# Whole-number comparison, one masking step and one sum in the top-16 selection of a hybrid encoder step

## The reference, cut to what matters

```python
v1, i1 = lax.top_k(s1, PEER_TOPK)
v2, i2 = lax.top_k(s2, PEER_TOPK)
cand_s = (v1[..., :, None] + v2[..., None, :]).reshape(T, PEER_HEADS, PEER_TOPK * PEER_TOPK)
cand_i = (i1[..., :, None] * N_KEYS + i2[..., None, :]).reshape(T, PEER_HEADS, PEER_TOPK * PEER_TOPK)
top_s, sel = lax.top_k(cand_s, PEER_TOPK)
e_idx = jnp.take_along_axis(cand_i, sel, axis=-1)
gate = jax.nn.softmax(top_s, axis=-1)
u = exp_u[e_idx]
act = jax.nn.gelu(jnp.einsum('thkd,td->thk', u, h).astype(jnp.float32), approximate=False)
return jnp.einsum('thk,thkd->td', (gate * act).astype(h.dtype), exp_v[e_idx])
```

## Time and profile before

| | us |
|---|---|
| median of 3 runs | 1144.43 |
| lowest and highest | 1144.29, 1145.9 |
| the profiled execution, time | 1144.88 |
| its span | 1143.1 |

### The profile page before, as it was taken

One profiled execution on the slowest core, in us unless ns is written; L12 is line 12 of the kernel. 1 busy time (PEld: TensorE's weight loads), 2 busy tenths in 40 slices (PEclk: granted clock), 3 DMA queues, 4 the chain that ended last, 5 costly groups with the idle time before them and its releaser, 6 DMA issues.

```text
span 1143.1 us, 12068 instructions
## 1 busy us (share of the span) xinstructions
PE 856.5 (75%) x3879; PEld 396.3 (35%) x3884; DVE 784.8 (69%) x2005; ACT 454.8 (40%) x1423; POOL 536.3 (47%) x437
## 2 busy tenths in 40 slices
PE   8999988997896858685686777587666756655555
PEld 6748743443232424241243442143223222211111
DVE  2325877876677888796666786757877777667554
ACT  2121454333444334552564663343343333333334
POOL 0002445553555554553553553556564654455442
PEclk9999999999999888897889898889898788887879
DMA  9902999999999999999999999999999999999996
GB/s 375 411 2 70 421 425 425 427 424 430 425 427 425 426 428 426 361 430 422 425 427 425 425 427 427 425 426 427 426 427 426 427 427 428 427 425 427 427 428 269
DMA packets 66791, 456.60 MB, mean 399 GB/s; under 512 B 8227, under 2 KB 10019, under 8 KB 15526
## 3 DMA queue, kind: packets, MB, share of 16 engines
q0 software_dynamic: 55888, 402.68, 83.8%
q1 hardware_dynamic: 10694, 52.87, 11.4%
q10 hardware_dynamic: 144, 0.26, 0.1%
HBM read 451.49 MB, written 3.24 MB: 398 GB/s over the span
## 4 chain that ended last, share of the span: by engine, by line
DMA 48%; PE 26%; DVE 11%; POOL 7%; ACT 4%; issue 3%; SPq 0%; POOLq 0%; DVEq 0%
DMA rows<-in_uv,ids 37%; PE ps L598 25%; DMA wt<-in_uv,ids 8%; DVE rows L2043 6%; POOL rows L537 4%; POOL work L520 2%; DMA wt<-in_uv,last_ids 1%; DMA rows<-in_w_qi 1%; ACT work L1249 1%; ACT wt L1249 1%; DMA wt<-in_w_q 1%; ACT wgt L1249 1%; DVE wt L2043 1%; PE ps L601 1%; ACT zact L1249 1%
## 5 line engine op out<-in xcount | busy, mean ns | idle before, releaser
L537 POOL DMA_INDIRECT rows<-in_uv,ids x352 | 400.3, 1137 | 444.9 <-PE ps L598 360.7
L598 PE MATMUL ps<-rows,work 128*64 128x512 f32 x1416 | 409.4, 707 | 245.2 <-ACT work L1249 239.7
L2043 DVE CUSTOM_DVE_ANT_0 rows<-rows,wt 128x1024 f32<-128x1024 f32 x226 | 276.9, 1225 | 160.9 <-DMA rows<-in_uv,ids 155.7
L1249 ACT ACTIVATE zact<-zdot 128x1 f32<-128x1 f32 x354 | 71.6, 202 | 488.2 <-DVE zdot L2043 480.5
L598 PEld LDWEIGHTS ps<-rows,work 128*64 128x64 f32 x1416 | 96.2, 151 | 479.3 <-ACT work L1249 327.3
L598 PE MATMUL ps<-wt 128*128 128x128 f32 (+6 forms) x719 | 195.9, 476 | 30.4 <-ACT wt L1249 28.1
L2043 DVE CUSTOM_DVE_ANT_0 rows<-rows,masks 128x1024 f32<-128x1024 f32 x128 | 156.3, 1224 | 67.3 <-DMA rows<-in_uv,ids 64.5
L598 PEld LDWEIGHTS ps<-wt 128*128 128x128 f32 (+2 forms) x724 | 97.8, 185 | 106.6 <-issue 58.8
L1249 ACT ACTIVATE work<-pair,wgt 128x64 f32<-128x64 f32 x354 | 123.4, 349 | 11.5
L1249 ACT ACTIVATE wgt<-zact,gates 128x1 f32<-128x1 f32 x354 | 104.5, 295 | 11.6
L598 PEld LDWEIGHTS ps<-work,wt 128*128 128x128 f32 (+1 forms) x664 | 84.2, 202 | 48.6 <-issue 48.2
(11 more groups left out here) (178 smaller groups left out, 722.9 us busy)
## 6 DMA issues: line engine op xcount, KB each, us to landing
wt<-in_w_q SPq DMA_DIRECT2D x7, 2048.0 KB, 15.9
rows<-in_uv,ids POOLq DMA_INDIRECT x352
rows<-in_w_out SPq DMA_DIRECT2D x2, 2048.0 KB, 32.5
wt<-in_w_out SPq DMA_DIRECT2D x2, 2048.0 KB, 12.0
wt<-in_ckv SPq DMA_DIRECT2D x16, 256.0 KB
x<-in_x SPq DMA_DIRECT2D x5, 512.0 KB, 8.9
rows<-in_w_qi SPq DMA_DIRECT2D x1, 2048.0 KB, 13.3
wt<-in_w_qa SPq DMA_DIRECT2D x1, 2048.0 KB, 12.5
```

The costliest lines, as they stand in the source:

```text
L537: pool.indirect_dma_start(row[s], None, a["uv"], bass.IndirectOffsetOnAxis(ap=ids[:, own(n // KP).start + n % KP:own(n // KP).start + n % ...
L598: return nc.tensor.matmul(out, lhsT, rhs, start=start, stop=stop)
L1249: return nc.scalar.activation(*args, **kw)
L2043: V.tensor_tensor_reduce(row[s][:, 0:D], row[s][:, 0:D], h2r[t][:, n % 2, :], 1.0, 0.0, ALU.mult, ALU.add, zdots[s]).then_inc(dotted, 1)
```

## The change

- `topi` stays whole numbers: the cast to `topf` is gone. Its first half is shifted left by 7 (times 128) in place, by an instruction that is put behind the first maximum of the sums, with one wait for both.
- The shift, the mask and the cast of `besti` become one masking instruction, `besti` against the constants 240 and 15 (`nibble`, set at the start). The comparison is with 0, 16, .. 240 for the first half and 0..15 for the second (`iota`, now 2 x 16 and in another place).
- The one-hot table is multiplied by `topi` and summed over both halves and the last axis at once, straight into `flat`.
- Unit 0 posts `chosen` when its ids are there and again when its gates are; PE spreads them in two batches (`spread_first`), DVE posts `picked` after the ids and again after the gates, and POOL's first gather waits for the ids alone. All later counts of `chosen`, `spread_ps` and `picked` go up by one.
- `post` is `across` without the wait. It is used for `smax`, `pscaled` and the ids of units 1 to 23.

```diff
-        iota = sb("iota", [P, KP])
-        topf = at(work, 4000, 32).rearrange("p (e k) -> p e k", e=2)
+        nibble = at(work, 4000, 2).bitcast(U32)
-        rankf = at(work, 4096, 32).rearrange("p (e k) -> p e k", e=2)
-        half_id = at(work, 3840, 32).rearrange("p (e k) -> p e k", e=2)
+        iota = at(work, 4096, 32).rearrange("p (e k) -> p e k", e=2)
...
                 if n % KP == 0:
-                    pool.wait_ge(picked, n // KP + 1)
+                    pool.wait_ge(picked, n // KP + 2 if n else 1)
...
+            def spread_first():
+                pe.wait_ge(q_sb, 1)
+                for k in range(2):
+                    pe.wait_ge(chosen, k + 1)
+                    for j in range(2):
+                        for q in range(2):
+                            last = mm(spread_psum(k)[64 * q:64 * q + 64, j * KP + k * 8:j * KP + k * 8 + 8], ident[:, 64 * j:64 * j + 64],
+                                      flat[0].rearrange("p e (c q) -> p e q c", q=2)[:, k, q, :])
+                    last.then_inc(spread_ps, 1)
...
             sums_1(1)
-            spread_out(0)
+            spread_first()
             sums_1(2)
...
+            def post(ins, s):
+                key = s.name
+                count[key] = count.get(key, 0) + 1
+                ins.then_inc(s, 1)
+                yield
...
             def top16_pairs(u):
-                then(V.tensor_copy(topf, topi))
                 c4 = cand.rearrange("p (i j) -> p i j", i=KP)
...
-                then(V.max(out=best[:, 0:8], in_=cand))
+                V.max(out=best[:, 0:8], in_=cand).then_inc(chain, 1)
+                V.tensor_scalar(topi[:, 0, :], topi[:, 0, :], 7, None, ALU.logical_shift_left).then_inc(chain, 1)
+                count[chain.name] += 2
+                dve.wait_ge(chain, count[chain.name])
...
             def top16_ids(u):
-                V.tensor_scalar(rank[:, 0, :], besti, 4, None, ALU.logical_shift_right)
-                then(V.tensor_scalar(rank[:, 1, :], besti, 15, None, ALU.bitwise_and))
-                yield from across(V.tensor_copy(rankf, rank))
-                yield from across(V.tensor_tensor(hot, rankf.rearrange("p e (k a) -> p e k a", a=1).broadcast_to([P, 2, KP, KP]),
-                                                  iota[:].rearrange("p (e a r) -> p e a r", e=1, a=1).broadcast_to([P, 2, KP, KP]),
+                yield from across(V.tensor_tensor(rank, besti.rearrange("p (e k) -> p e k", e=1).broadcast_to([P, 2, KP]),
+                                                  nibble.rearrange("p (e k) -> p e k", k=1).broadcast_to([P, 2, KP]), ALU.bitwise_and))
+                yield from across(V.tensor_tensor(hot, rank.rearrange("p e (k a) -> p e k a", a=1).broadcast_to([P, 2, KP, KP]),
+                                                  iota.rearrange("p e (a r) -> p e a r", a=1).broadcast_to([P, 2, KP, KP]),
                                                   ALU.is_equal))
-                yield from across(V.tensor_tensor(hot, hot, topf.rearrange("p e (a r) -> p e a r", a=1).broadcast_to([P, 2, KP, KP]),
+                yield from across(V.tensor_tensor(hot, hot, topi.rearrange("p e (a r) -> p e a r", a=1).broadcast_to([P, 2, KP, KP]),
                                                   ALU.mult))
-                yield from across(V.tensor_reduce(half_id, hot, AX.X, ALU.add))
-                V.scalar_tensor_tensor(flat[u % 2][:, 0, :], half_id[:, 0, :], float(NK), half_id[:, 1, :], ALU.mult, ALU.add).then_inc(chain, 1)
-                count[chain.name] += 1
+                ids_of = V.tensor_reduce(flat[u % 2][:, 0, :], hot.rearrange("p e k r -> p k e r"), AX.XY, ALU.add)
+                if u == 0:
+                    ids_of.then_inc(chosen, 1)
+                else:
+                    yield from post(ids_of, chain)
...
             def spread_take(u):
-                dve.wait_ge(spread_ps, u + 1)
+                dve.wait_ge(spread_ps, u + 2 if u else 1)
                 src = spread_psum(u).rearrange("p (j e c) -> p e c j", j=2, e=2)
-                V.tensor_copy(ids[:, own(u)].rearrange("p (c j) -> p c j", j=2), src[:, 0, :, :])
-                if u >= 1:
-                    dve.wait_ge(picked, u)
+                ins = V.tensor_copy(ids[:, own(u)].rearrange("p (c j) -> p c j", j=2), src[:, 0, :, :])
+                if u == 0:
+                    ins.then_inc(picked, 1)
+                    dve.wait_ge(spread_ps, 2)
+                    src = spread_psum(1).rearrange("p (j e c) -> p e c j", j=2, e=2)
+                dve.wait_ge(picked, u + 1)
                 V.tensor_copy(gates[:, own(u)].rearrange("p (c j) -> p c j", j=2), src[:, 1, :, :]).then_inc(picked, 1)
...
             then(V.memset(ident_bf[:], 0.0), blank)
+            for i, bits in enumerate((240, 15)):
+                ins = V.memset(nibble[:, i:i + 1], bits)
+            then(ins)
```

## The result

The changed kernel took **1158.06 us** (1157.85 to 1158.81), the kernel before 1144.98 in the same comparison. The ratio is 1.0115, with a 95% interval of 1.0097 to 1.0132. The forecast was 1143.6 with a range to 1145.6, so it was wrong, in size and in sign. The profiled execution took 1158.14 us, with a span of 1156.2 (1143.1 before). One of the ten executions of the kernel with the wide table, further down, took 2667.09 us and is left out of its ratio and range.

The account below looks back on a forecast made before the run. Transfer bytes at 427 GB/s were taken to set the end from about 111 us on. 1144.88 less 0.60 (start) and 0.2 (hole) gave 1144.1 for the profiled execution, 1143.6 us as a median, range 1141.4 to 1145.6.

Parts of the forecast that it names:

- the hole: Window from 400 to 500 us at 408 GB/s, 4.4 us of transfer missing; forecast to stay, with 0.2 us gained.
- its own signs of being wrong: Forecast wrong if the 400 to 500 us dip is gone or doubled, or the other windows' rate has moved.
- DVE's terms in unit 0: At the start: cast gone saves 0.21 us, shift costs 0.08, mask 0.22 saves 0.28; conversion free, sum 0.69.
- the bounds of the head: First gather 0.60 us earlier; 0.8 with cheap matmuls, 1.3 were PE no bound, nothing if mask and sum were dear.
- the dear ends of mask and sum: DVE in unit 0: mask at 0.46 us instead of 0.22, and the sum 0.75 us longer from its input order.
- PE as the bound of the spreading: At the start, PE is busy with tile 1's index scores until 108.13; ids wait for it, spreading starts 0.51 us earlier.
- Everything behind it shifts: At the start: DMA engines are empty until the first gather, so bringing it forward (0.60 us) shifts everything behind it.
- rival 1: Head gain spent before the steady stage, or new forms dear: 1144.2 us, chance 0.14.
- Rival 4: A second hole at tile 1's norm after lookup 47, costing 4.4 us: 1148.0 us, chance 0.06.
- rival 3: The dip at 400 to 500 us mostly closes, both PE pairs at full clock, 2.6 us less: 1141.0, chance 0.12.
- the tail: Stretch behind the last gather; the change was said not to touch it.

Follow-up runs that it names:

- the kernel with the wide table: Kernel before, with the constant table in HBM 32 columns wide and half of it loaded; SBUF addresses and instructions unchanged: 1144.6 us, ratio 0.9999.
- the kernel before with the shift alone: Kernel before, with the table of 0..15 put in the work buffer, moving all large buffers down 64 bytes: 1159.62 us, ratio 1.0135.
- the run with the gates waited for: Changed kernel plus the 64-byte buffer, with PE's batches and POOL's first gather waiting for unit 0's gates again: 1143.1 us, ratio 0.9986.
- the moved batch: Changed kernel plus the 64-byte buffer, with PE's first spreading batch ahead of the second group of index scores: 1144.35 us, ratio 0.9994.
- four buffers moved: Changed kernel with four small buffers (192 bytes) allocated behind the large ones, so the ring starts at 32256: 1142.78 us, ratio 0.9981.
- the power earlier: Changed kernel plus the 64-byte buffer, with POOL's power for tile 2's norm taken behind gather 125, not 126: 1143.9 us, ratio 0.999.

## Why the prediction was wrong, step by step

- **The bound was read rightly, and its rate was taken for a constant.** The prediction found that bytes at 427 GB/s set the end, and then looked only for what could start them earlier or leave holes. The rate is the largest term of all: 1.4% of it is 15.2 us. The step that failed is the one that isn't there: all 100 us windows outside the hole were to stay "at 425 to 427 GB/s". The diff showed a buffer of 64 bytes taken away, and the prediction put it at nothing without a reason; its terms were instructions and waits only. Measured, the quiet windows stood at 421, and the kernel with the buffer put back (15.2 us faster) and the kernel before with the shift alone (14.7 slower than before) show that this is the whole of the loss. The last of its own signs of being wrong, that the rate in the other windows has moved, is the one that came.
- **DVE's terms in unit 0 were right.** Mask 0.22 us as taken, shift 0.07 (0.54 us from the start of the first maximum to the masking out of its values, 102.06 to 102.60, where it was 0.47), conversion and order of the sum free. The rule of the Trainium skill ("Vector Engine (DVE) Microarchitecture Reference", section "Measured stream behaviour on trn2") on runs of adjacent words holds in this trace: the sum took 0.69. In the bounds of the head the prediction says "nothing" for the dear ends of mask and sum and then works out 0.3; its own figures give 0.3. DVE was busy 774.2 us, 773 had been forecast.
- **PE as the bound of the spreading was right**, as the run with the gates waited for shows. The first gather came 0.60 us earlier by the change, as worked out. PE's work behind it was to come 0.17 earlier and came 0.28, since the two batches took 0.57 us from start to start and not 0.68.
- **"Everything behind it shifts" was wrong.** The first gather moved alone (0.27 us in one run, 0.44 in the other) brought nothing that can be told; with 0.44, POOL's gathers behind it came later. This is rival 1, the head gain spent before the steady stage, for about half of the 0.60. From 110 to about 150 us PE's program sets the pace. The gain at the start comes because PE's next work starts earlier, 0.5 us: 108.98 before, 108.46 with the buffer put back, of which 0.24 is the head start of that execution and 0.28 the change's.
- **The hole's price was wrong.** It was read as 4.4 us that are missing. Taking DVE's wait away closed it and saved nothing that can be told; the moved batch nearly closed it too, and saved nothing. Rival 4 was priced at those 4.4 us, and rival 3 at 2.6 of them.
- **The size of the change itself** was 0.8 us by the forecast and is 1.7 by the run with the buffer put back (0.7 to 2.7), and 2.2 by the one with four buffers moved, whose other changes are addresses alone. Of the forecast's two terms, 0.60 for the head and 0.2 for the hole, 0.28 of the first holds, so about 1 us is not accounted for by name. The traces show where the rest lies, not why. One place is the window from 400 to 500 us: 413, 412 and 412 GB/s in the kernels with the buffer, with four buffers behind and with the gates waited for, and 408 and 410 in the kernel before and the one with the wide table, which is 0.8 us. The other is the tail, which the prediction put at nothing: in the last of the 40 slices the same three have 278, 279 and 278 GB/s and the same two 269 and 263, which is another 0.8 us.

## What to carry to other kernels

Where transfers set the end, look at the addresses they write to before looking at the engines: print the start of every large buffer, and keep them at multiples of 256 bytes, since any small buffer that is added, dropped or resized moves all that are allocated behind it. Two traces that have the same DMA share, near 1, and a different rate do not differ by a wait of the transfers; here no engine's order had a part in it. A hole in a full stretch is worth its price only once a run without it is faster; here another opened in its place. And before a slow row beside a hole is called its cause, look for the same row in a trace that has no hole there.

The version to keep is the changed kernel with its large buffers on the line: 1142.84 us with 64 unused bytes, or 1142.78 with four small buffers allocated last, against 1144.88 and 1144.75 for the kernel before in the same comparisons.

## What the runs showed of the hardware that was not expected

- A start in SBUF 64, 128 or 192 bytes past a multiple of 256 lowers the rate of full transfers, rows of 8 KB, from 427 to 421 GB/s, all three alike. At 224 past (no multiple of 64) it was 420, and the time 3 to 4 us longer again.
- It goes by each transfer's own destination. With the ring off the line and the buffers behind it on it, the first loads ran at 424, as in the kernels with both on it (422 to 425; 416 to 418 with both off it), and the gathers, mostly into the ring, at 423.
- After 5.96 to 7.34 us without work PE ran a pair of lookups in 3.68 us instead of 1.94 at about 720 us, in the kernel before, with the gates waited for and with the power earlier (granted clock 0.50, the 1.2 GHz level, from 720 to 724 us). In the first two it cost the transfers nothing: 425 and 422 GB/s from 720 to 740 us.
